# A residual-split fp32r matmul stream: the weights' low-part tile placed 64 bytes further, and the activation tiles placed on one 512-byte phase

## What is computed

```
proj = h @ w_in                     # 2048 -> hybrid projections
... @ w_out,  h @ sc_w_in,  (y*silu(z)) @ sc_w_out
h @ w_in_2, ..., relu(h @ w_ff1)**2 @ w_ff2
```

## The kernel before, in words

| tile | start before, modulo 512 | after, modulo 512 |
|---|---|---|
| raw | 128 | 128 |
| wh | 128 | 128 |
| wl | 128 | 192 |
| xs | 128 | 128 |
| hid, hid2 | 64 | 128 |
| wab2 (in hid) | 64 | 128 |

## Time and profile before

### The profile page before, as it was taken

The page is one execution under the profiler, slowest core; times in us unless marked ns, Lnnn a source line. Parts: engine busy times, 40 slices in busy tenths (PEclk is TensorE's granted clock), DMA queues, the critical chain, the costliest instruction groups (busy, mean ns, idle before and its releaser), DMA issues.

```text
span 3023.3 us, 51503 instructions
## 1 busy us (share of the span) xinstructions
PE 2953.2 (98%) x17546; PEld 2572.6 (85%) x17546; DVE 2152.5 (71%) x3020; ACT 1506.3 (50%) x2164; POOL 452.1 (15%) x187
## 2 busy tenths in 40 slices
PE   7999999999999999999998999999999999999998
PEld 6889898889987888888887877788887888888887
DVE  6666666676568888888877899876687426565465
ACT  4454444544444444444444777766544444444443
POOL 0111011110100000000000000000002445545443
PEclk9999999999999999999998999999999999999999
DMA  6444434444457887888885545456785566766655
GB/s 214 143 138 132 136 131 142 139 139 146 147 192 254 311 298 282 317 303 303 301 294 172 166 168 168 166 194 211 246 303 172 188 210 223 243 236 236 206 182 174
DMA packets 172690, 629.41 MB, mean 208 GB/s; under 512 B 19224, under 2 KB 20376, under 8 KB 171808
## 3 DMA queue, kind: packets, MB, share of 16 engines
q1 hardware_dynamic: 165024, 601.99, 57.6%
q10 hardware_dynamic: 7552, 25.91, 2.5%
HBM read 615.22 MB, written 12.60 MB: 208 GB/s over the span
## 4 chain that ended last, share of the span: by engine, by line
PE 69%; issue 24%; DVE 4%; ACT 2%; DMA 1%; DVEq 0%; POOL 0%; SPq 0%; ACTq 0%; POOLq 0%
PE gemm L537 42%; PE gemm L542 21%; PE side L670 1%; PE side L677 1%; DVE wl L1520 1%; ACT wh L976 1%; PE side L682 1%; PE side L563 0%; DMA raw<-in_stream 0%; DMA x<-in_x 0%; PE side L737 0%; DVE gB L1711 0%; ACT gA L1078 0%; DVE xs L1599 0%; PE side L714 0%
## 5 line engine op out<-in xcount | busy, mean ns | idle before, releaser
L537 PE MATMUL gemm<-xs,wh 128*128 128x512 f32 x5120 | 1649.6, 404 | 28.7 <-DVE xs L1599 8.6
L976 ACT ACTIVATE wh<-raw 128x1024 fp32r<-128x1024 f32 x939 | 984.4, 1058 | 925.9 <-PE gemm L542 799.6
L1520 DVE TENSOR_TENSOR wl<-raw,wh 128x1024 fp32r<-128x1024 f32 x811 | 1035.7, 1281 | 451.2 <-ACT wh L976 428.7
L542 PEld LDWEIGHTS gemm<-xs,wl 128*128 128x128 f32 x5120 | 967.1, 189 | 229.4
L542 PE MATMUL gemm<-xs,wl 128*128 128x256 f32 x5120 | 1013.2, 279 | 0.0
L537 PEld LDWEIGHTS gemm<-xs,wh 128*128 128x128 f32 x5120 | 786.4, 190 | 56.5 <-issue 50.8
L537 PE MATMUL gemm<-hid,wh 128*128 128x512 f32 x2368 | 748.5, 397 | 6.7 <-DVE fxg L1525 2.2
L542 PEld LDWEIGHTS gemm<-hid,wl 128*128 128x128 f32 x2368 | 446.8, 189 | 102.0
L542 PE MATMUL gemm<-hid,wl 128*128 128x256 f32 x2368 | 468.8, 279 | 0.0
L1449 POOL TENSOR_TENSOR wl<-raw,wh 128x1024 fp32r<-128x1024 f32 x128 | 348.8, 2730 | 370.5 <-ACT wh L976 370.5
L537 PEld LDWEIGHTS gemm<-hid,wh 128*128 128x128 f32 x2368 | 358.4, 189 | 9.7 <-ACT wh L976 3.3
(11 more groups left out here) (377 smaller groups left out, 1951.4 us busy)
## 6 DMA issues: line engine op xcount, KB each, us to landing
raw<-in_stream SPq DMA_DIRECT2D x940, 512.0 KB, 3.8
ada_a<-in_ada SPq DMA_DIRECT2D x144, 512.0 KB, 5.0
ada_b<-in_ada SPq DMA_DIRECT2D x48, 512.0 KB, 5.1
stash<-stage ACTq DMA_DIRECT2D x12, 512.0 KB, 3.0
att<-stash ACTq DMA_DIRECT2D x8, 384.0 KB, 4.0
x<-in_x SPq DMA_DIRECT2D x4, 512.0 KB, 5.7
xacc<-in_x ACTq DMA_DIRECT2D x1, 2048.0 KB, 11.2
stash<-stA ACTq DMA_DIRECT2D x4, 512.0 KB, 6.5
```

The source lines that it names most:

```text
L537: mm(G[n][:, :], wh[:, slot, at:at + P], rhs(sl * SLAB_K + k), start=sl == 0 and k == 0, stop=False, skip_group_check=True)
L542: op = mm(G[n][:, T:2 * T], wl[:, slot, at:at + P], rhs(sl * SLAB_K + k)[:, 0:T], start=False, stop=last, skip_group_check=True)
L976: A(wh[:, slot, :], raw[:, slot, :], ACT.Copy).then_inc(hi_ready, 1)
L1520: tt(wl[:, slot, :], raw[:, slot, :], wh[:, slot, :].bitcast(F32), ALU.subtract).then_inc(lo_ready[slot], 1)
```

## The change

It moves tiles and nothing else: no instruction is added, removed or put in another order. `nrm` and `rn` (64 bytes together) are placed between `wh` and `wl`; `mod` and `norm_g` (448 bytes together) between `wl` and `xs`; and 64 bytes are left free ahead of `hid`. `tmp`, `vec`, `cst` and `xs` move by 512 bytes, `parts`, `hid` and all that is placed from `hid`'s end by 64. The low halves' tile is `wl`, the norm's output is `xs`.

```diff
     raw = place("raw", [P, RING, SLAB])
+    wh_at = top[0]
     wh = place("wh", [P, RING, SLAB], F32R)
+    nrm = place("nrm", [P, 8])
+    rn = place("rn", [P, 8])
+    wl_at = top[0]
     wl = place("wl", [P, RING, SLAB], F32R)
+    mod = place("mod", [P, 96])
+    norm_g = place("norm_g", [P, KC])
     xs_at = top[0]
     xs = place("xs", [P, KC, 2 * T], F32R)
     tmp = place("tmp", [P, 4, T])
     vec = place("vec", [P, VEC_N])
     cst = place("cst", [P, CST_N])
-    mod = place("mod", [P, 96])
-    norm_g = place("norm_g", [P, KC])
     parts = place("parts", [P, 2 * 96])
-    nrm = place("nrm", [P, 8])
-    rn = place("rn", [P, 8])
     mhalf = place("mhalf", [P, 8])
     dnh = place("dnh", [P, 8])
+    top[0] += (wh_at - top[0]) % 512
     hid_at = top[0]
+    assert (xs_at - wh_at) % 512 == 0 and (hid_at - wh_at) % 512 == 0 and (wl_at - wh_at) % 512 == 64
     hid = place("hid", [P, 24, 2 * T], F32R)
```

## The result

| | before | changed |
|---|---|---|
| median | 3022.53 us (4 runs, 3021.52 to 3024.36) | 3039.04 us (4 runs, 3033.36 to 3042.80) |
| profiled execution | 3025.32 us | 3033.36 us |
| ratio, 95% interval | | 1.0050 [1.0037, 1.0063] |

The forecast was 3013.0 us and faster. The changed kernel took 3039.0, 26 us more than forecast and 16.5 us more than before: inside the range of 2993 to 3048, but on the other side of no change. The changed kernel's own runs spread over 9.4 us, those of before over 2.8.

A forecast was written before the change was run, and what follows sets the result against it. TensorE, 98% busy, was taken as the bound. Gemm groups gave -8.7 us, other terms about 0: 3025.3 to 3016.6 us for the profiled execution, 3013.0 against the median; 8-in-10 range 2993 to 3048.

The forecast's parts named there:

- The splits' term: VectorE's split writing `wl` at its new address: bounds -62 to +62 ns a slab, cost taken as 0.
- g: Time of one gemm group of matmuls, claimed equal on `xs` and `hid` after the change; forecast 693.4 ns.
- I take -8.7: Chosen gemm saving in us: groups on `xs` fall from 696.8 to 693.4 ns, `hid` unchanged.
- Three cases: Observed distances from activations to weights: 0 on `xs` (696.8 ns), +64 on `hid` (693.4), -64 at the gates.
- the linear middle (695.1): Gemm group time in ns if each weight load counts by itself: -2.4 us in all.
- The third case: The gates' 16 wide matmuls on `xs`, weights at -64: 229.4 ns each, read as cheaper than at distance 0.
- the slower rival: Mixed distances dearer than either pure case in all 3744 gemm groups: over 3028 us, chance 0.26.
- Priced at 703: Upper-end gemm group time in ns, second wide matmul dear and first not cheap: +27 us.
- all 3744 groups: Gemm groups counted at full effect, 2560 on `xs` and 1184 on `hid`; each nanosecond a group is 3.7 us.

The follow-up runs named there:

- k2: Before, with only `hid` moved 64 bytes up, so that all distances from activations to weights are 0: 3024.3 us, against 3023.4 for before beside it.
- k3: Before, with `xs` moved down to 64 modulo 512, where `hid` is, weights unmoved: 3019.9 us, against 3023.4 for before.
- k7: Before, with both weight tiles starting at 384 instead of 128 modulo 512, `xs` and `hid` on their old phases: 3019.3 us, against 3020.4 for before.
- k10: Before, with high weights at 192, low weights at 256, `xs` at 256, `hid` still at 64 (modulo 512): 3038.8 us, against 3023.5 for before.
- k16: The changed kernel as it is, timed again in more rounds: 3040.85 us, ratio 1.0057 to before.
- k4: Before, with only the high weights moved, starting at 192 instead of 128 modulo 512: 3058.4 us, against 3023.4 for before.
- k9: Before, with both weight tiles at 0 and `xs` and `hid` at 64 modulo 512, all distances -64: 3011.77 us, ratio 0.9959.
- k8: Before, with only the low weights moved, starting at 64 instead of 128 modulo 512: 3034.8 us, against 3020.4 for before.

## Why the prediction was wrong, step by step

**Right: what bounds the kernel, and that place alone acts.** The group time from start to start was the thing to read, the distances the thing to count (k2, k3 and k7 to 0.1 ns), and the two runs came out equal. The splits' term, set to 0, was 0 (1280 ns against 1281).

**Wrong: which g.** The step that failed is "I take -8.7. Of three cases the only dear one has all distances 0, and the change leaves no group with all at 0". It took the dearness of (0, 0) as a property of distance 0, and any other distance as a cure. The table shows none of this: (0, 0) is among the cheap ones, and (64, 0) and (128, 0) are dearer by 10 to 16 ns. Three cases, all with equal distances, held nothing on unequal ones, and the linear middle (695.1) failed for the same reason.

**The third case was misread.** "Both nonzero distances are cheaper than 0" set the gates, which have wide matmuls only, against groups that mix wide and narrow ones. The change puts the gates at distance 0, and k10 at +64 (modulo 256). The timelines of the changed kernel and, behind the dots, of k10:

```profile
59.17 3.81 PE L610 MATMUL side<-xs,wab 128*128 128x512 f32 x16
62.83 0.61 PE L541 MATMUL gemm<-xs,wh 128*128 128x512 f32 x2
...
58.91 3.89 PE L606 MATMUL side<-xs,wab 128*128 128x512 f32 x16
62.63 0.63 PE L537 MATMUL gemm<-xs,wh 128*128 128x512 f32 x2
```

3.66 us / 16 = 228.8 ns each at 0 (the prediction charged 233.4 there), 232.5 at +64, against 229.4 at -64. In this row of wide matmuls alone, 0 isn't dear and +64 is, the reverse of the groups, where +64 is 3.4 ns cheaper than 0 (693.4 against 696.8). At distance 0 the gates' matmuls are as cheap as at -64, so their case didn't support the step.

**The mechanism was on the list, as the slower rival, and only half priced.** It said that the second wide matmul stays dear, as on `hid`, while the first no longer gets its cheapness. Distances from start to start, averaged over the uninterrupted groups at their usual length:

| | first wide | second wide | first narrow | second narrow | group |
|---|---|---|---|---|---|
| hid before (64, 64) | 225.9 | 235.7 | 118.3 | 113.3 | 693.4 |
| changed (0, 64), both tiles | 232.3 | 235.8 | 118.4 | 113.5 | 700.0 |

Three of the four are `hid`'s of before; the first wide matmul, beside which the second high block loads, costs 6.4 ns more. (In the changed kernel's timeline two high blocks load from 2661.87 us on, 0.19 us each and 0.30 together, so the second loads from 2661.98 on, when the first wide matmul starts.) This describes one pair of distances in one of its rhythms and is no rule: k16's groups of 706.7 ns have 235.0, 233.3, 121.7 and 116.7, and k4 refuted the rule. Priced at 703 it gave 3049 us; at 700.0 it is 2560 x 3.2 + 1184 x 6.6 = 8.2 + 7.8 = +16.0 us, 3038, which the median of 3039 meets. That agreement is partly luck, since two effects offset each other: the second rhythm adds, and not every group counts.

**How much reaches the end.** The forecast took all 3744 groups. Small matmuls are hooked into many of them, and such an interrupted group, with what stands in it, hardly changes: in the hybrid stage's 768 groups on `xs`, 496 are interrupted and take 1089 ns in the mean before, 1089 in the changed kernel (495) and 1088 in k9. Uninterrupted there are 1863 on `xs` and 1036 on `hid`, with means of 696.9 and 693.8 before, 690.5 and 690.5 in k9: 1863 x -6.4 + 1036 x -3.3 ns = -15.3 us, and k9's span is 15.3 us below before's. The 21 us were mis-sized by counting interrupted groups. That the two figures meet to 0.1 us is luck: k7 has the group times of before, and its span is 6.0 us below before's, 3.2 of them in the 480 groups on `xs` that start at 1612 and 1614 us (418.9 us against 422.1). The medians' 11.7 us are less again, as the profiled execution of before stands 1.9 us above its median and k9's 1.8 below. A part of what the groups gain also goes into waits: TensorE's idle time adds up to 60.7 us before and to 66.1 in k9. For the changed kernel the same sum gives 1863 x 4.3 + 1036 x 7.0 = +15.3 us in its first profile, whose span rose by 8.0 only, and 1863 x 6.4 + 1036 x 9.6 = +21.9 in k16, with 17.3. In the MLP the runs from 2290 us on last 4.6 us more, of 5.0 expected; what is missing lies in the interrupted groups of the earlier stages. TensorE's idle time fell by 2.2 us (60.7 to 58.5), and the rest is no more than k7 and before differ by at equal group times. Which wait gave it back wasn't settled.

Shown is the dependence: with nothing but placement, g goes from 690.0 (k9) to 713.3 ns (`hid` in k8). Why it has these values stays open. No run took the weight loads away, so whether they hinder the moving stream wasn't shown.

## What to carry to other kernels

Where TensorE streams fp32r matmuls back to back, read the time from start to start; the modelled durations show little (404 ns on `xs` in both kernels, while the group went from 696.8 to 700.0). In this kernel it depends on where the weight tiles begin relative to the moving tile, and 256 bytes more left it as it was (k7): from 690 to 713 ns a group, 3%, at no cost in instructions. Of that, the best placement gave 0.4% of the kernel's time over the one of before. Measure the placement that you mean to use, since neither its parts nor its neighbours tell its price, nor does another mix of matmuls (the gates), and profile it more than once, as one placement can have two rhythms (700.0 and 706.7 ns here).

## What the runs showed of the hardware that was not expected

- The time of this stream of fp32r matmuls depends on tile starts. It repeated at 256 bytes: k7's distances of 256 and 320 gave 696.8 and 693.4 ns, as 0 and 64 did before. 32 bytes already matter: equal distances (modulo 256) of 0, 32, 64, 96, 128, 160, 192, 224 give 696.7, 702.7, 693.4, 703.3, 696.8, 706.7, 690.0 and 693.4 ns.
- The sign counts: -64 is 3.3 ns cheaper than +64 (690.0 against 693.3), (64, 0) 15 ns dearer than (-64, 0) (713.1 against 698.3).
- The means over runs of 128 groups often lie on steps of 3.33 ns (690.0, 693.3, 696.7, 700.0, 703.3, 706.7), but not always (698.3, 702.7, 704.9). Single groups can alternate: in k9 688 and 692 ns in turn, in k8 on `xs` 700, 690 and 690.
- The gates' 16 wide matmuls alone take 228.8 ns each at 0 (changed kernel), 229.4 at -64 (before), 232.5 at +64 (k10); the groups' order is another: 696.7, 690.0, 693.4.
- The same program settles in a 700.0 or a 706.7 ns rhythm and keeps it for hundreds of groups (670 at 700 in the changed kernel's first profile, 760 at 706.7 in k16).
